# Second block: attention, recurrence and attention norm placed between the input panels, head by head; rotary turns and splits of the first block placed inside their neighbouring stages

## What is computed

```
h    = rmsnorm(x, g_mix) * (1 + sc1) + sh1
proj = h @ w_in                       # q, k, v: 8 heads of 128; f: 8 logits; lx, ly: 1024 columns each
logits = q k^T * scale + cum(log_sigmoid(f + b_f))_q - cum(...)_k, causal   # 8 heads, 256 tokens
attn = softmax(logits) v
xc   = causal_conv4(lx)
r, i = sigmoid(xc @ w_a + b_a), sigmoid(xc @ w_x + b_x)      # 8 blocks of 128x128
a    = exp(-8 r softplus(-lam));  h_t = a_t h_(t-1) + sqrt(1 - a_t^2) * i_t * xc_t
lru  = h * gelu(ly)
x   += ga1 * (concat(rmsnorm(attn, g_attn), rmsnorm(lru, g_lru)) @ w_out)
```

## Time and profile before

| | |
|---|---|
| median of 3 runs | 3735.68 us (3734.17 to 3736.08) |
| the profiled execution's own time | 3738.8 us |
| its span, first to last instruction | 3737.1 us |
| PE busy | 84% |
| DVE busy | 67% |
| ACT busy | 31% |
| granted TensorE clock, mean | 0.91 |

### The profile page before, as it was taken

How to read it: one execution, slowest core, us unless ns; L and a number is a source line. 1 busy time by engine, 2 the same in 40 slices (tenths; PEclk the granted TensorE clock), 3 DMA queues, 4 the chain that set the end, 5 groups by cost and what they waited for, 6 DMA issues and landing times.

```text
span 3737.1 us, 39190 instructions
## 1 busy us (share of the span) xinstructions
PE 3130.6 (84%) x14772; PEld 2358.0 (63%) x14772; DVE 2504.1 (67%) x3403; ACT 1153.2 (31%) x1749; POOL 597.4 (16%) x692
## 2 busy tenths in 40 slices
PE   6699998988979989997999689999999984545555
PEld 1488875446758886486997589787887861112222
DVE  4988876746776656455562554777777855778775
ACT  1421225133242343244442443344443430111101
POOL 0000000000100000000000000111111126666662
PEclk9899999989979999898996799999999997777777
DMA  8555760524866763354651234898997968889996
GB/s 350 211 217 226 267 259 1 185 86 181 314 236 249 284 221 124 146 200 168 219 182 38 108 137 175 323 371 309 384 367 309 355 264 302 349 345 361 357 362 262
DMA packets 146983, 915.92 MB, mean 245 GB/s; under 512 B 21617, under 2 KB 30065, under 8 KB 40433
## 3 DMA queue, kind: packets, MB, share of 16 engines
q0 software_dynamic: 75776, 503.47, 35.4%
q1 hardware_dynamic: 56912, 384.82, 26.8%
q10 hardware_dynamic: 14112, 25.17, 1.8%
HBM read 884.03 MB, written 29.36 MB: 244 GB/s over the span
## 4 chain that ended last, share of the span: by engine, by line
PE 60%; DVE 20%; DMA 6%; PEld 5%; issue 4%; ACT 2%; another core or an unknown queue 1%; POOL 0%; DVEq 0%; SPq 0%; ACTq 0%; PEldq 0%; POOLq 0%
PE psum L896 29%; PE psum L869 17%; DVE psum L1642 7%; PEld psum L896 5%; PE psum L973 5%; PE psum L903 5%; DVE junk L1380 2%; PE psum L990 2%; DMA memr<-in_ada_dram 2%; DMA memr<-in_peer_v_dram,memr 2%; DMA memr<-in_panels_dram 1%; PE psum L981 1%; DVE w_lo L1073 1%; PE psum L914 1%
## 5 line engine op out<-in xcount | busy, mean ns | idle before, releaser
L1073 DVE TENSOR_TENSOR w_lo<-memr,w_hi 128x1024 fp32r<-128x1024 f32 x614 | 740.0, 1222 | 457.9 <-ACT w_hi L1067 456.7
L1067 ACT ACTIVATE w_hi<-memr 128x1024 fp32r<-128x1024 f32 x614 | 641.8, 1056 | 954.9 <-PE psum L896 317.4
L1380 DVE CUSTOM_DVE_ANT_0 junk<-memr 128x2048 bf16<-128x2048 f32 x256 | 585.7, 2288 | 126.5 <-DMA memr<-in_ada_dram 85.5
L896 PE MATMUL psum<-h_hi,w_hi 128*128 128x512 f32 (+1 forms) x1696 | 602.4, 355 | 70.0 <-DVE h_lo L1451 47.8
L896 PE MATMUL psum<-h_lo,w_hi 128*128 128x512 f32 (+1 forms) x1696 | 590.3, 348 | 0.0
L896 PE MATMUL psum<-h_hi,w_lo 128*128 128x512 f32 (+1 forms) x1696 | 590.3, 348 | 0.0
L1012 PE MATMUL psum<-memr,memh 128*128 128x512 f32 x520 | 323.3, 780 | 311.3 <-DMA memr<-in_peer_v_dram,memr 198.1
L1012 PEld LDWEIGHTS psum<-memr,memh 128*128 128x128 f32 x520 | 126.0, 254 | 508.2 <-issue 428.6
L869 PE MATMUL psum<-w_hi,l_hi 128*128 128x512 f32 x1024 | 403.5, 394 | 28.6 <-DVE w_lo L1073 28.6
L869 PE MATMUL psum<-w_hi,l_lo 128*128 128x512 f32 x1024 | 402.2, 393 | 0.0
L896 PEld LDWEIGHTS psum<-h_hi,w_hi 128*128 128x128 f32 x1696 | 325.4, 192 | 121.4 <-issue 66.8
(11 more groups left out here) (182 smaller groups left out, 3816.2 us busy)
## 6 DMA issues: line engine op xcount, KB each, us to landing
memr<-in_panels_dram SPq DMA_DIRECT2D x339, 1024.0 KB, 6.4
memr<-in_ada_dram POOLq DMA_DIRECT2D x176, 1024.0 KB, 5.9
dots<-sq ACTq DMA_DIRECT2D x64, 256.0 KB
memr<-in_xin_dram SPq DMA_DIRECT2D x1, 4096.0 KB, 14.1
gstore<-sq ACTq DMA_DIRECT2D x16, 256.0 KB
memh<-gstore SPq DMA_DIRECT2D x2, 2048.0 KB, 8.0
memr<-gstore SPq DMA_DIRECT2D x2, 2048.0 KB, 10.1
memr<-in_xin_dram SPq DMA_DIRECT2D x2, 2048.0 KB, 7.3
```

What stands on the lines that cost most here:

```text
L896: ins = pe.matmul(bank(o["bank"])[:, 0:o["w"]], w_[:, c, :], x_[:, kc, :], start=kc == 0 and j == 0, stop=kc == DC - 1 and j == 2)
L1067: act.activation(w_hi[:, m % HALVES, :, :], slot[:, 8 * i:8 * i + 8, :], ACT.Copy).then_inc(hi_ready, 1)
L1073: dve.tensor_tensor(w_lo[:, m % HALVES, :, :], raw_panel(o["g"])[0][:, 8 * i:8 * i + 8, :], w_hi[:, m % HALVES, :, :].bitcast(F32), ALU.su ...
L1380: chain(dve.tensor_tensor_reduce(junk[:, :], w, cact[:, v_, :], 1.0, 0.0, ALU.mult, ALU.add, mod[:, a, m:m + 1]))
```

## The change

In the second block the panels now come in the order f, lx (8), then q, k, v of one head after the other with the gate panel between q and k of head 0, then ly (8). `pe_mix`, `act_mix` and `dve_mix` run the whole of it as one stage: after the eight lx the convolution is done and the gates' eight outputs are made; the recurrence runs in seven steps on DVE behind the following outputs; the two attention units of head h follow its v; its turns and values follow one output and two outputs later; the norm of the attention half, its rounding and its remainders lie behind the ly outputs. A small stage `mixed` is left for the last chunk, the norm of the other half and its rounding. The cumulative logits go in as one product with 40 rows (`f_cols`, `f_rows`) in place of two or three with 8 rows. The dense outputs use three PSUM banks instead of four. The x for the residual is loaded in two halves: the upper one when the mixed stage begins, the lower one when it ends.

In the first block the `norm` stage with the four rotary tiles is gone: the swaps come after outputs 5, 7, 9, 11 of the up projections, the turns after 7, 9, 11, 13. The `split` stage is gone: each head's output is rounded one and two units after it is taken. The third condition vector is waited for at the end of layer 0's second attention, and the wait for the gates comes before the first head is taken.

```diff
-    for kind, n in (("q", 8), ("k", 8), ("v", 8), ("f", 1), ("lx", 8), ("ly", 8), ("lru", 1), ("out", DC),
-                    ("pq", DC), ("pk", 1), ("u", N_EXP // P)):
+    panels += [(2, "f", 0)] + [(2, "lx", i) for i in range(8)]
+    for i in range(HEADS):
+        panels += [(2, "q", i)] + [(2, "lru", 0)] * (i == 0) + [(2, "k", i), (2, "v", i)]
+    panels += [(2, "ly", i) for i in range(8)]
+    for kind, n in (("out", DC), ("pq", DC), ("pk", 1), ("u", N_EXP // P)):
...
+            st["ropes"] = [dict(rope=qr[:, i, S:T2], pair=1, sw=totals["swap"] + i, of=st["outs"][i]) for i in range(4)]
...
-            norm([dict(x=[], stat=False, rope=qr[:, i, S:T2], pair=1) for i in range(4)],
-                 post=None if layer else "c2")
...
+            st["post"] = None if layer else "c2"
+            st["split"] = [(Y2[:, h, lo:T2], h_hi[:, 8 + h, lo:T2], h_lo[:, 8 + h, lo:T2], totals["xh"] + h) for h in range(8)]
...
-        stage("load_x", x=X2, src="xstore", part=0, engines=("sp",))
+        stage("load_x", x=X2[:, 8:16, :], src="xstore", part=1, engines=("sp",), after=mixed["k"])
+        stage("load_x", x=X2[:, 0:8, :], src="xstore", part=0, engines=("sp",))
...
+            for p_, o in enumerate(st["outs"]):
+                if o.get("lru") == 0:
+                    pe.wait_ge(conv_ready, 8)
+                pe_output(pe, o, st["norm"]["groups"][0]["xl"] if p_ == 0 else None)
+                if unit_at(p_ - 2):
+                    turn(unit_at(p_ - 2))
+                if unit_at(p_ - 3):
+                    values(unit_at(p_ - 3))
+                if unit_at(p_):
+                    score(unit_at(p_))
+                if p_ - 1 in head_place:
+                    turn_values(head_place[p_ - 1])
+                if LY0 + 3 <= p_ < LY0 + 6:
+                    for c in range(3 * (p_ - LY0 - 3), min(3 * (p_ - LY0 - 2), HEADS)):
+                        pe_squares2(pe, 0, c)
+                if p_ >= LY0 + 6:
+                    for c in range(3):
+                        pe_squares2(pe, 1, 3 * (p_ - LY0 - 6) + c)
...
-            for p_, o in enumerate(st["outs"]):
-                while j < min(2 * p_ + 5, len(halves_)):
+            held = next((o for o in st["outs"] if "lru" in o and o["last"]), None)
+            for o in st["outs"]:
+                while j < min(2 * split + 5, len(halves_)):
+                    if held and o["n"] <= held["n"] and halves_[j][0]["g"] >= held["g"] + SLOTS:
+                        break
...
+                if p_ == LY0 + 5:
+                    act_root2(act, 0, chain)
...
+                if p_ == LY0 + 6:
+                    act_rounded2(act, 0)
+                    for i in range(2):
+                        act_half(act, st["next"]["outs"][0], i)
...
+            def taken(o):
+                p_ = o["n"] - st["outs"][0]["n"]
+                if unit_at(p_ - 2):
+                    normalise(unit_at(p_ - 2))
+                if unit_at(p_ - 1):
+                    maximum(unit_at(p_ - 1))
...
+                recurrence(p_ - gates_done - 2)
+                for j in range(o["ada"]):
+                    ada_chunk(dve, o["ada0"] + j, chain)
+                if p_ >= LY0 + 1:
+                    dve_gated(dve, p_ - LY0 - 1)
```

More of the change, by code:

```diff
@@ L501, in build @@
-        vouts = [o for o in st["outs"] if 16 <= o["g"] - g < 24]
-        add(st, [dict(turn=[v2T[:, 4 * b + j, P * t:P * t + P] for j in range(4)], after=vouts, eng="VA"[b],
-                      dst=v2[:, t, 4 * b:4 * b + 4, :], view="p (j d) -> p j d", act=ACT.Copy)
-                 for t in range(2) for b in range(2)])
-        g += 41
-        units = []
+            if kind == "lru":
+                return [dict(groups=[((0, S), [(ring[:, slot, 2 * n, :], xc[:, n, :])]),
+                                     ((S, T2), [(ring[:, slot, 2 * n + 1, :], xc[:, n, :])])],
+                             eng="A", lru=n) for n in range(8)]
@@ new lines, in in2 @@
+            head = qkv[:, i % 2, :, :]
+            dst = {"f": fl, "lx": lx[:, i, 3:LXW], "ly": Y[:, 8 + i, :], "q": head[:, 0, :], "k": head[:, 1, :],
+                   "v": head[:, 2, :]}[kind]
+            return [dict(x=(l_hi, l_lo), w=S, eng="A", dst=dst, act=ACT.Gelu_apprx_tanh if kind == "ly" else ACT.Copy,
+                         kind=kind, i=i)]
+        mix = gemm(g, 42, in2)
+        mix["mix"] = True
+        for p_, o in enumerate(mix["outs"]):
+            o.update(bank=p_ % 3, banks=3)
@@ L523, in build @@
-        gemm(g, 1, lru)
-        g += 1
-        stage("scan", engines=("act", "dve"))
-        norm([dict(x=[Y[:, i + c, :] for c in range(8)], w=1024, gain=[(gain, c) for c in range(8)],
-                   hi=halves["hi"][i:i + 8], lo=halves["lo"][i:i + 8]) for i, gain in ((0, "g_attn"), (8, "g_lru"))])
+                mix["units"].append(dict(h=h, qt=qt, nk=P * (qt + 1), n=totals["unit"], hn=totals["head"]))
+                totals["unit"] += 1
+            totals["head"] += 1
+        mixed = stage("mixed", engines=("pe", "act", "dve"))
@@ L597, in build @@
         for st in stages:
+            if st["kind"] == "mixed":
+                st["next"] = mix["next"] = next(s_ for s_ in stages[st["k"]:] if s_["kind"] == "gemm")
+                st["next"]["norm"] = st
             if st["kind"] == "norm" and "hi" in st["groups"][0]:
@@ L610, in begin @@
         def begin(eng, me, st):
-            upto = st["norm"]["k"] if me == "pe" and "norm" in st else st["k"]
+            upto = st["norm"]["k"] if me == "pe" and "norm" in st else st.get("after", st["k"])
             for e in ("pe", "act", "dve"):
@@ L1261, in act_forget, with act_square2 @@
             act.activation(lt, lt, ACT.Ln, bias=one_t[:, :]).then_inc(lam_ready, 1)
-        def act_scan(act, st, chain):
-            act.wait_ge(la_ready, 1)
-            act.activation(lru_e, ga, ACT.Exp)
-            act.activation(lru_t, ga, ACT.Tanh).then_inc(th_ready, 1)
-            act.wait_ge(bt_ready, 1)
-            act.activation(lru_t, lru_t, ACT.Sqrt, scale=-1.0).then_inc(bs_ready, 1)
+        def act_square2(act, group, c):
+            gr = mixed["groups"][group]
+            n = gr["sq0"] + c
+            if group == 0:
+                act.wait_ge(o_used, mix["units"][2 * c]["hn"] + 1)
+            else:
+                act.wait_ge(lru_gated, c + 1)
+            act.wait_ge(sq_used, n - 3)
+            act.activation(squares2[n % 4], Y[:, gr["first"] + c, :], ACT.Square).then_inc(sq_ready, 1)
@@ new lines, in act_root2, with act_rounded2 @@
+        def act_root2(act, group, chain):
+            gr = mixed["groups"][group]
+            act.wait_ge(sq_used, gr["sq0"] + 8)
+            act.wait_ge(normed, gr["ms"])
+            chain(act.activation(rinv2, sums_bank2(group), ACT.Ln, bias=eps_t[:, :], scale=1.0 / 1024))
+            act.activation(rinv2, rinv2, ACT.Exp, scale=-0.5).then_inc(rinv_ready, 1)
+        def act_rounded2(act, group):
+            gr = mixed["groups"][group]
+            for c in range(8):
+                act.wait_ge(xn_ready, gr["xn"] + c + 1)
+                act.activation(m_hi[:, gr["first"] + c, :], Y[:, gr["first"] + c, :], ACT.Copy).then_inc(xh_ready, 1)
@@ L1517, in take, with remainder @@
                 o = bank(O_BANK + u["hn"] % 2)[:, u["out"][0]:u["out"][1]]
[L1518 to L1523 removed]
+                dve.tensor_tensor(u["y"], o, u["gate"], ALU.mult).then_inc(o_used, 1)
+            def remainder(h):
+                x, hi, lo_, n = st["split"][h]
+                dve.wait_ge(xh_ready, n + 1)
+                dve.tensor_tensor(lo_, x, hi.bitcast(F32), ALU.subtract)
+            taken = 0
+            for i in range(len(us) + 6):
                 if i < len(us):
@@ L1572, in top16, with dve_mixed @@
+        def dve_mixed(dve, st, chain):
+            dve_gated(dve, 7)
+            scaled, remainder = dve_scaled2(dve, 1, chain)
+            for c in range(10):
+                if c < 8:
+                    scaled(c)
+                if c >= 2:
+                    remainder(c - 2)
+            dve_normed2(dve, 1)
         def top16(dve, link, s, sb_, v, ix):
@@ L1760, in _arrays @@
         else:
-            panels.append(_panel(part[kind], n))
+            panels.append(_panel(part[kind], out_chunk(n) if kind == "out" else n))
     panels = np.stack([p.reshape(P, PANEL) for p in panels])
```

491 lines of the change are left out of this document (342 added, 149 removed).

## The result

The changed kernel takes 3682.2 us (median of 4 runs, 3677.7 to 3689.2) against 3735.9 of the kernel before on the same chip (4 runs, 3734.2 to 3745.7): ratio 0.985, interval 0.983 to 0.988, 54 us less. The forecast was 3651, the range 3630 to 3690. So the gain is 54, 64 and 72 us in three sets of runs; 84 had been forecast.

What follows compares the result with a forecast made beforehand. PE sets the dense pace; a serial piece costing 127 us could be filled. Second block 127 - 49 - 16 = 62, first block 22.4, total 84.4: 3738.8 - 84.4 = 3654.4, median 3.1 lower, 3651 us; range 3630 to 3690 (8 in 10).

Steps and rivals of the forecast that it cites:

- First block: Both layers' second attention: earlier scores gain 13.8 and 4.0 us, earlier rounding at the ends 2.0 and 2.6; sum 22.4.
- The rival that had the clock stay up: Layer 1's attention starts at full clock, up to 9 us; chance 0.12 shared with a shorter tail; 3625 to 3642.
- Between the panels: Second block: work and waits put among the 41 dense outputs cost 28 + 7.0 + 6.1 + 5.0 + 3 = 49 us.
- attention, 8 heads: Second block: scores, logits, masks, turns and values between dense outputs, 3.6 us a head at full clock, 28 taken.
- gates: Second block: 16 gate products of 256 columns at 0.437 us, 7.0 us; 1.9 more for low clock after a gap.
- squares: Second block: 14 of the 16 sum-of-squares products lie behind ly outputs, 14 x 0.437 = 6.1 us.
- waits: Second block: PE idle 3.1 us after k of head 0, and 3 us over 16 softmax turns at 0.2 each.
- Softmax late at every step: Rival, second block: in-order ACT and DVE delay all 16 turns; 13 to 40 us, 3664 to 3695; chance 0.15.
- The clock falls inside the mixed run: Rival, second block: small products bring PE's lower clock for good, 165 us lost against 84 gained, 3732 to 3760; chance 0.05.
- Convolution (2.0 a panel) beside 2.44 fits in 5.72: Second block, lx panels: DVE's convolution and remainders fit within one panel's PE time, so no PE time is charged.
- A new wait: Second block: v of head 0 waits for the gate panel's slot, leaving PE idle 3.1 us after k of head 0.
- The tail: After the last input output: 15.9 us to the mixed stage's end, then 11.4; two panels return 11.4, net cost 16.

Runs made afterwards that it cites:

- e4: Kernel before with only the first block's edits, second block as before: 3665.4 us against 3689.8 for the kernel before, 24.5 us less.
- e5: The changed kernel again, unedited, on a second chip: 3678.6 us against 3742.9 for the kernel before, ratio 0.9816.
- e10: Changed kernel with only x's lower half loaded behind two more output panels: time equal to e9's.
- e6: Changed kernel with the half panels of k of head 0 held back on ACT and DVE until the seventh gate output: median 9.6 us less than e5's.
- e12: Changed kernel with panel held until seventh gate output, recurrence three outputs later, later modulation chunks, x's lower half later: median 15.4 us below e9.
- e1: Changed kernel with the half panels of k of head 0 held back on ACT and DVE until the first gate output: ratio 0.981 to the kernel before.
- e9: The changed kernel again, unedited, on a third chip: 3613.8 us against 3686.0 for the kernel before, ratio 0.9795.

## Why the prediction came out 30 us too good

The direction, the mechanism and most of the terms held; the time lies in the range for 8 in 10, near its slow end, and outside the forecast's own range of 3640 to 3664, which had been given 0.65. By the changed stretches the gain was 69.9 instead of 84.4: 14.5 us of the miss are the forecast's. The rest, 20 us in the profiled execution, lies in unchanged stretches. 9.6 of it is the start-up, which differs as much between executions with nothing changed there; why the others were longer stays open. In three sets of runs the gain varied from 54 to 72, so the size of the miss is in part chance.

**First block, forecast 22.4, measured 23.7 in the trace and 24.5 in e4.** Layer 0: 13.8 forecast, 13.85 measured. Its end: 2.0 forecast; from the last rounding (872.22) to the first dense product (878.86) it is 6.6 us, 1.7 less than in the earlier trace rows. But the attention before it is 1.6 longer, since the clock stays low for longer (0.67 in the second twelve microseconds after its start, 0.81 before), so 0.1 is left. Layer 1: 4.0 forecast, 3.95 measured. Its end: 2.6 forecast, 5.8 measured, of which 2.4 lie between the last rounding and the first dense product, as forecast, and 3.4 in the attention before, where the lower clock lasts less (0.64 in the second twelve microseconds before, 0.91 now). So the sum came out right because two things that the forecast left out, 1.6 lost and 3.4 gained, nearly cancel. The rival that had the clock stay up came true in two of the thirteen profiles with this first block, e5's and e10's: e5's attention of layer 1 starts with 12 instructions in 6.37 us instead of 11.60, and takes 59.5 us to the output projection instead of 65.9.

**Between the panels, forecast 49, measured 73.1.** I add up PE's rows from the second dense output to the end of the last (1742.65 to 2047.69, 305.0 us; before 1749.00 to 1980.95 and 232.0), each instruction's time taken to the start of the next and waits apart:

```
                    forecast            measured
dense outputs       as before, 232.0    240.4 (+8.4)
attention, 8 heads  28                  29.0
gates               7.0 (+1.9 clock)    8.6
squares             6.1                 4.0
waits               3.1 + 3             23.1
```

- Attention: 28 was right to 4%, but single prices were not. A head's products with 40 rows took 1.04 us instead of 0.75, its scores 0.84 instead of 0.95 and its turns 0.51 instead of 0.65; that the sum of 3.6 held is luck in part.
- "Softmax late at every step" didn't happen: after head 0 the turns wait 0.2 to 0.5 us, near the 0.2 forecast. Head 0's 3.60 and 1.05 are over the 1 us that the forecast had named as a sign that it is wrong.
- "The clock falls inside the mixed run" didn't happen either: 1.00 over 179 us with small products among the large, 0.97 over the whole 305 us. Its price was wrong in the forecast: 165 us more than forecast would have been 3651 + 165 = 3816 us, not 3732.
- The step that failed is "Convolution (2.0 a panel) beside 2.44 fits in 5.72", with its "so nothing else is charged": an average load, where an order in time was needed. A convolution and a chunk stand between the two halves of one panel on DVE; the remainder behind them frees the slot late, the next panel is late too, and takes 6.9 to 8.6 us to load where a chunk's load was issued 0.5 us ahead of it, instead of 4.8, and by the last convolutions the panels' ring has no slack. That gave 4.7 us of waits at lx.
- "A new wait": I looked for it behind the gates, through the slot, and priced 3.1 us; it is 1.53 there, ended by DVE's remainder. The 11.0 us are in front of them, from work queued on DVE and ACT behind a panel that nobody needs yet. I had named what queues behind SP, not what queues behind ACT and DVE. e6 takes these 11 us away.
- Head 0's turns: 3.60 and 1.05 us instead of 0.2 each. The recurrence stands on ACT before the rounding; I had costed its steps on DVE only.
- The lower clock after gaps was priced once with 1.9 (the row it was read from gives 6.43 - 31 x 0.119 = 2.7); the dense outputs cost 8.4 more. In e12, with 3.6 us of waits in the same stretch instead of 23.1, they still cost 4.1 more: wherever other work comes between, the last product before it and the first after it take 0.21 us to the next instead of 0.12, and there are some 30 such places. The other 4.3 go with the gaps and the lower clock after them, by the same comparison.

**The tail, forecast 27.4 from the last input product to the third output panel, measured 23.45** (2047.69 to 2071.14). PE's wait of 1.44 us there is ended by DVE's remainder, but the chain behind it is a DMA, as forecast:

```profile
2061.58 7.08 DMA memr<-in_panels_dram
2068.68 1.07 ACT w_hi L1172
```

The mixed stage ends 13.5 us after the last input product (SP issues x's lower half at 2061.21), where 15.9 had been forecast, and from there it is 9.9 us to the product, where it was 11.4. The third output panel to the keys' product takes 195.8 us, 199.8 before; I had not counted that the projection no longer restarts at the low clock (its last row), which makes 2.5 of it (that panel's product takes 6.2 us, 8.7 before). The terms 62 - 24.1 + 3.95 + 4.0 = 45.9 give the measured gain of the second block, 46.2, but for rounding.

**ACT's table loads.** A load starts when the activation before it ends (1819.18 in e1's rows above, the load at 1819.20), 1.28 us, and the next activation follows at 1820.49; 14 of the 54 loads of the changed kernel stand so, with under 0.05 us on either side. The drain of the Trainium skill, page "ScalarE: Activation LUTs", section "What ACT_TABLE_LOAD costs", about 1.38 us a switch, is not seen here either.

## What to carry to other kernels

Before independent work is put between dense products, write down for each engine the order of its queue around the new work, and ask at each wait what stands behind it: a panel asked for one place too early cost 11 us of TensorE's time, while DVE and ACT, which had the work to release it, only waited for that panel. An average load per panel says whether the engines can keep up, not whether they do at the one place where a buffer is missing; look there at the order, and hold the early work back until what it blocks is done. Compare variants by the changed stretch as well as by the total, since the total of one kernel on one chip moved by up to 24 us from one execution to another (e5: 3666.7 to 3691.1).

## What the runs showed of the hardware

The same kernel is 53 to 65 us slower on one chip than on another: before 3742.9 on e5's and 3689.8 and 3686.0 on the two others, after 3678.6 and 3613.8. The difference lies in the last stage, where the DMA engines are busy for 0.90 of a window and more; its windows show (the changed kernel's first profile, then its profile e9 on the faster chip; the columns of the earlier trace rows):

```profile
3300.00:3450.00 150.00, 80.14 (x134) 31.20 (x132) 117.30 (x190) 14.26 (x30) 95.37 (x101) 0.78 0.90 352
```

```profile
3300.00:3450.00 150.00, 88.66 (x148) 34.48 (x147) 131.84 (x203) 16.15 (x34) 111.25 (x118) 0.82 1.01 409
```

352 and 409 GB/s; from the end of the product that starts at 2929.1 and 2916.9 us (84.7 us each) to the end of the span it is 673.6 and 606.4 us. That the transfers are the cause, and not another engine's work with them, is not shown.

How long TensorE stays at its lower clock after a short pause is not fixed by the kernel. In twelve of the thirteen profiles with the changed first block PE stands idle for 2.35 to 2.36 us before the second attention of layer 1. In the twelve microseconds from its start the granted clock was 1.00 in e5 and e10 and 0.50 to 0.54 in the ten others, 0.52 in the first profile of the changed kernel and in e9, with PE busy for all 12 us in these four.
